# Hybrid encoder layer on Trainium2: twelve gate projections moved into attention, softmax row sums taken from a block of ones

## The reference

```
z = rms_norm(x) @ w_in          # -> c_q 256 | c_kv 128 | k_r 32 | u 1024 | gate_a 1024 | gate_b 1024
q = rms_norm(c_q) @ w_q_b       # 16 heads x (64 + 32 rotary), normalised per head, rotated
kv = [past, rms_norm(c_kv)] @ w_kv_b     # 16 heads x (64 key + 64 value), keys normalised per head
attn = softmax(q k^T / sqrt(96), block causal, chunk 64) @ v           # branch A
u_c = causal conv of width 4 over u
r, i = sigmoid(u_c @ w_rg + b_rg), sigmoid(u_c @ w_ig + b_ig)          # 8 blocks of 128
a = exp(-8 r softplus(-lam));  h_t = a_t h_(t-1) + sqrt(1 - a_t^2) (i u_c)_t    # branch B
x = x + (sigmoid(gate_a) * attn + sigmoid(gate_b) * h) @ w_out
x = x + ConvFFN(rms_norm(x))    # w_up to 5632, conv of width 3, silu gate, w_down
```

## Time and profile before

| what | us |
|---|---|
| median of three runs (945.2, 946.52, 2200.45) | 946.52 |
| the profiled execution's own time | 945.21 |
| span of the profiled execution | 943.3 |
| TensorE busy | 899.4 (95%) |
| TensorE weight loads busy (beside the matmuls) | 847.8 (90%) |
| VectorE busy | 604.8 (64%) |
| ScalarE busy | 347.5 (37%) |
| GpSimd busy | 238.3 (25%) |

### The profile page before, as it was taken

One profiled execution on the slowest core, in us unless ns is written; L12 is line 12 of the kernel. 1 busy time (PEld: TensorE's weight loads), 2 busy tenths in 40 slices (PEclk: granted clock), 3 DMA queues, 4 the chain that ended last, 5 costly groups with the idle time before them and its releaser, 6 DMA issues.

```text
span 943.3 us, 18508 instructions
## 1 busy us (share of the span) xinstructions
PE 899.4 (95%) x6689; PEld 847.8 (90%) x6689; DVE 604.8 (64%) x1182; ACT 347.5 (37%) x619; POOL 238.3 (25%) x278
## 2 busy tenths in 40 slices
PE   5999999998799999998999999999999999999998
PEld 5899999987577887776799999999999999999998
DVE  4378634686789888897544488777778777322221
ACT  6331455364344444442423533333333332112111
POOL 4000233462333221331012233333333333201000
PEclk8999999999899999997999999999999999999999
DMA  8333323322000000010003232233332222233321
GB/s 256 79 84 76 97 78 82 77 73 46 15 7 10 14 14 14 20 27 1 1 23 90 67 110 78 81 88 89 89 89 82 78 85 84 84 97 104 98 70 36
DMA packets 114630, 63.55 MB, mean 67 GB/s; under 512 B 7836, under 2 KB 113054, under 8 KB 114588
## 3 DMA queue, kind: packets, MB, share of 16 engines
q1 hardware_dynamic: 112396, 59.17, 22.4%
q0 software_dynamic: 2192, 3.81, 1.8%
HBM read 59.85 MB, written 2.70 MB: 66 GB/s over the span
## 4 chain that ended last, share of the span: by engine, by line
PE 86%; DVE 6%; issue 4%; ACT 2%; POOL 1%; SPq 1%; DMA 0%; DVEq 0%; ACTq 0%; POOLq 0%
PE PS L1141 61%; PE PS L1354 4%; PE PS L1338 4%; PE PS L1319 3%; PE PS L1176 3%; PE PS L1265 2%; PE PS L1308 2%; PE PS L1214 2%; PE PS L1261 1%; PE PS L1362 1%; PE PS L1292 1%; PE PS L1283 1%; DVE small L1010 1%; DVE w_lo L773 0%; PE PS L1325 0%
## 5 line engine op out<-in xcount | busy, mean ns | idle before, releaser
L541 ACT ACTIVATE w_hi<-w_raw 128x1024 fp32r<-128x1024 f32 (+2 forms) x104 | 107.6, 1035 | 368.7 <-PE PS L1141 354.4
L773 DVE TENSOR_TENSOR w_lo<-w_raw,w_hi 128x1024 fp32r<-128x1024 f32 (+2 forms) x104 | 128.1, 1231 | 122.8 <-ACT w_hi L541 122.6
L1141 PE MATMUL PS<-x2h,w_hi 128*128 128x274 f32 x704 | 147.7, 291 | 1.1 <-DVE w_lo L773 1.1
L1141 PE MATMUL PS<-x2h,w_lo 128*128 128x274 f32 x704 | 146.9, 290 | 0.0
L1141 PE MATMUL PS<-x2l,w_hi 128*128 128x274 f32 x704 | 146.9, 290 | 0.0
L1141 PEld LDWEIGHTS PS<-x2h,w_hi 128*128 128x128 f32 x704 | 111.9, 189 | 1.4 <-issue 1.3
L1141 PEld LDWEIGHTS PS<-x2l,w_hi 128*128 128x128 f32 x704 | 112.0, 189 | 0.0
L1141 PEld LDWEIGHTS PS<-x2h,w_lo 128*128 128x128 f32 x704 | 111.4, 189 | 0.0
L1141 PE MATMUL PS<-xnh,w_hi 128*128 128x274 f32 x384 | 83.3, 299 | 4.4 <-DVE w_lo L773 2.3
L1141 PE MATMUL PS<-xnl,w_hi 128*128 128x274 f32 x384 | 81.7, 295 | 0.0
L1141 PE MATMUL PS<-xnh,w_lo 128*128 128x274 f32 x384 | 81.0, 293 | 0.0
(11 more groups left out here) (254 smaller groups left out, 1706.6 us busy)
## 6 DMA issues: line engine op xcount, KB each, us to landing
w_raw<-in_w_up_dram SPq DMA_DIRECT2D x44, 512.0 KB, 3.8
w_raw<-in_w_in_dram SPq DMA_DIRECT2D x24, 512.0 KB, 3.9
w_raw<-in_w_down_dram SPq DMA_DIRECT2D x16, 512.0 KB, 3.7
w_raw<-in_w_out_dram SPq DMA_DIRECT2D x8, 512.0 KB, 4.1
w_raw<-in_w_down_dram SPq DMA_DIRECT2D x8, 384.0 KB, 3.9
xnat<-in_x_prompt_dram SPq DMA_DIRECT2D x4, 512.0 KB, 5.0
w_raw<-in_w_in_dram SPq DMA_DIRECT2D x4, 416.0 KB, 4.7
wq<-in_w_q_b_dram SPq DMA_DIRECT2D x8, 192.0 KB, 2.5
```

The source lines that it names most:

```text
L541: nc.scalar.activation(hi[:, slot % 2, 0:n], raw[:, slot % 4, 0:n], ACT.Copy).then_inc(s_hi, 1)
L773: tt(lo[:, slot % 2, 0:n], raw[:, slot % 4, 0:n], hi[:, slot % 2, 0:n].bitcast(F32), ALU.subtract).then_inc(s_lo, 1)
L1141: last = mm(PS[:, 2 * rank + j, 0:HT], w[:, slot % 2, cols], x[:, k0 + k, j * HT:(j + 1) * HT], start=(k0 + k == 0 and first), stop=(k0 + ...
```

## The change

The w_in items are reordered and split. Twelve stay ahead of attention (`FIRST`: gates A and B of block 0, the eight U, gates A and B of block 1). The twelve gate items of blocks 2 to 7 become fill inside attention: two a pair for the first five pairs, one for pairs 5 and 6. Each is done as two `gate_half`s of 24 matmuls, one half of the tokens each, in steps 3 and 4 (first item) and 7 and 8 (second). Gate sigmoids become tanh(x/2) on ScalarE with the factor 1/2 and the 1 added elsewhere.

The whole recurrence, with its LRU products, is moved to the stage of the U items. The first tap of the convolution is done by ScalarE. GpSimd's order there is written out: besides the recurrence it holds the squares and the rotation for pairs 0 and 1.

Row sums no longer come from ScalarE's accumulator. V has a third slot between its two heads, a block of ones; the stationary operand of a values matmul is one head's V and the ones, 128 columns, so the other head's 64 rows of PSUM receive the row sums. The reciprocal and the diagonal of every step are gone; the turn is a plain transpose against the identity, and waits for the exps. ScalarE copies the sums of a head out (`head_sums`), VectorE takes the reciprocal of 128 x 548 of them in two halves at steps 1 and 2 of the next pair (`sums_inverse`), and GpSimd multiplies and adds (`mix`).

In each step the turn and the values stand directly behind the scores, ahead of the fill. Scores use two banks in place of three. The attention loop is written out for all eight pairs. Of the w_out items the first two do seven of their eight blocks of k, then the last block each (in `output_product`).

```diff
-I_LAT, I_IN, I_OUT = 0, 4, 28
+FIRST = [("A", 0), ("B", 0)] + [("U", n) for n in range(KD)] + [("A", 1), ("B", 1)]
...
+def fills(p):
+    return [I_G + 2 * p, I_G + 2 * p + 1] if p < 5 else [I_G + 5 + p] if p < 7 else []
...
+            def gate_half(item, j):
+                pe.wait_ge(s_lo, item + 1)
+                for k in range(KD):
+                    cols = slice(k * P, (k + 1) * P)
+                    for w, x, first in ((hi, xnh, True), (hi, xnl, False), (lo, xnh, False)):
+                        last = mm(PS[:, j, 0:HT], w[:, item % 2, cols], x[:, k, j * HT:(j + 1) * HT],
+                                  start=(k == 0 and first), stop=(k == KD - 1 and w is lo))
+                last.then_inc(s_used if j else s_gp, 1)
...
-                pe.wait_ge(s_dg, p * 9 + (n + 1))
+                pe.wait_ge(s_e, p * 9 + (n + 1))
...
-                    last = mm(bank[:, a * P:(a + 1) * P], Pn[:, n % 3, a * P:(a + 1) * P], dg[:, n % 3, :], start=True, stop=True)
+                    last = nc.tensor.transpose(bank[:, a * P:(a + 1) * P], Pn[:, n % 3, a * P:(a + 1) * P], ident[:, :])
...
-                        last = mm(PS[h * VD:(h + 1) * VD, 3, t * P:(t + 1) * P], V[:, par, a, h, :], PT[:, b, a * P:(a + 1) * P],
-                                  start=(a == 0), stop=(a == t))
+                        last = mm(values_bank(h)[:, t * P:(t + 1) * P], V[:, par, a, h:h + 2, :].rearrange("p h n -> p (h n)"),
+                                  PT[:, b, a * P:(a + 1) * P], start=(a == 0), stop=(a == t))
...
+                    transpose_probs(p, n)
+                    if n:
+                        values(p, n - 1)
+                    if kq and n == 0:
...
+                    if following and n == 3:
+                        for v in range(2):
...
+                            transpose_kq(p + 1, v, v)
+                        pe.wait_ge(s_trf, 5 * (p + 1) + 1)
+                        gate_half(first, 0)
+                    if following and n == 4:
+                        pe.wait_ge(s_trf, 5 * (p + 1) + 2)
+                        gate_half(first, 1)
...
+                    if second and n == 7:
...
+                        gate_half(second, 0)
...
-                    transpose_probs(p, par, n)
-                    if n:
-                        values(p, par, n - 1)
...
+            def head_sums(p, h):
...
+                nc.scalar.activation(sums[rows(h), 0:SEQ], values_bank(h)[rows(1 - h), :], ACT.Copy).then_inc(s_sum, 1)
...
+            def sums_inverse(p, j):
...
+                ins = nc.vector.reciprocal(sums[:, cols], sums[:, cols])
...
+            for n in range(4, KD):
+                square_a(n)
+            rotate(0)
+            for n in range(4, KD):
+                lru_input(n)
+            squares_keys(1)
+            squares_queries(1)
...
             pool.wait_ge(s_rec, KD)
+            nc.gpsimd.memset(V[:, :, :, 1, :], 1.0).then_inc(s_clear, 1)
```

More of the change, by code:

```diff
@@ L139, in layer @@
         xT = fixed("xT", [P, KD, T])
-        rs_at = place
         rsT = fixed("rsT", [P, T])
@@ L369, in _ @@
+            for t in range(I_OUT + 6, I_UP):
+                w_out_item(t)
             with sp.Fori(0, NU // 4) as it:
@@ L1066, in _ @@
-            attend(6, 0)
-            attend(7, 1)
+            dve.wait_ge(s_rec, KD)
+            for p in range(NP_):
+                attend(p)
+            sums_inverse(7, 0)
+            sums_inverse(7, 1)
+            dve.wait_ge(s_ri, NP_)
+            o_p, h_p = gate("A", 7), U[:, 7, LEAD:]
+            dve.wait_ge(s_o, 3 * NP_)
+            link(tt(o_p, o_p, sums[:, :], ALU.mult))
+            dve.wait_ge(s_hb, NP_)
+            tt(h_p, h_p, o_p, ALU.add).then_inc(s_mix, 1)
+            mixed_lo(7)
@@ new lines, in _, with output_product @@
+            pe.wait_ge(s_rope4, 48)
+            pe.wait_ge(s_mask, 16 * 8)
+            scores(0, 0)
+            scores(0, 1)
+            pe.wait_ge(s_clear, 2)
+            for p in range(NP_):
+                attend(p)
+            def output_product(r, k0, nk):
+                for k in range(k0, k0 + nk):
+                    pe.wait_ge(s_ml, k + 1)
+                    cols = slice(k * P, (k + 1) * P)
+                    for w, x, first in ((hi, mxh, True), (hi, mxl, False), (lo, mxh, False)):
+                        for j in range(2):
+                            last = mm(PS[:, 2 * r + j, 0:HT], w[:, r, cols], x[:, k, j * HT:(j + 1) * HT],
+                                      start=(k == 0 and first), stop=(k == KD - 1 and w is lo))
+                return last
```

1037 lines of the change are left out of this document (603 added, 434 removed).

## The result

The changed kernel takes 976.6 us (median of four runs, 975.3 to 977.7) against 945.9 for the kernel before (one of whose four runs took 2200 and is left out of the ratio): 1.033 times as long, 95% interval 1.031 to 1.035. It is slower by 31 us. The forecast was 959.5, slower by 14 and most likely "no change"; the time lies inside the range of 917 to 978, at its upper end.

The account below looks back on a forecast made before the run. TensorE was taken to bound nearly everywhere, so gains come only where it stands. Attention's start 187.5, attention 302.8, the rest 465.4 and a 1.9 wait give 957.6 of span, plus 1.9 around it: 959.5 us, range 917 to 978.

Parts of the forecast that it names:

- the walk of 69.9 us: U stage, engine by engine from 116.3 to GpSimd's ones at 186.2; with 1.3 of half clock, attention begins at 187.5.
- product 8: Ninth of the twelve w_in products ahead of attention, numbered from 0 in FIRST order; forecast to begin at 116.3.
- the stop at product 2: Third w_in product: its w_lo stands behind latent norms and tiles on VectorE, put at 3.8 us.
- My check: End of U stage: GpSimd's own work of 37.3 us gives a floor of 169.4, with 17 us of waits in the walk.
- A pair: Attention, pair with two gate items: 38.8 us of TensorE work plus waits of 2.4 and 1.7, 42.9 us.
- VectorE's chain with the two reciprocals in it: Attention, pair start to first key columns: 14.1 us, against TensorE at the gate half after 11.7; wait 2.4.
- rival 2: Attention: VectorE and GpSimd hold each other up at the shared port, 2.5 us a pair, 977 us; chance 0.24.
- Pair 0: First attention pair, with no reciprocals: forecast at 42.1 us.
- product 10: Eleventh w_in product ahead of attention, in the U stage: forecast to begin at 133.7.
- The end of attention: w_out item 2 waits for item 0's last block and pair 7's mix, behind two reciprocals: 1.9 us; then 465.4 as before.
- Rival 1: U stage and attention: engines overlap better, attention starts near 173 and takes 278.8, total 919 us; chance 0.27.
- Rival 3: Attention: reciprocals take only 0.47 us, the first wait goes in five pairs, 948 us, no change; chance 0.11.

Follow-up runs that it names:

- tail2: Changed kernel with the end of the U stage reordered, and the recurrence of blocks 4 to 7 ahead of pair 0 on shared engines: 968.2 us, ratio 1.025.
- combined2: Changed kernel with U stage reordered as in tail2, gate B half first, later w_lo of second items, earlier w_lo for product 2, w_out reordered: 922.5 us, ratio 0.977.
- half-first run: Changed kernel with each pair's first gate half ahead of the turns of keys, the other turn ahead of the second half: 970.3 us, ratio 1.027.
- exps_early: Changed kernel with ScalarE's exps of blocks 0 to 3 at the end of step 7 of FIRST: 974.1 us, ratio 1.031.
- no_recip: Changed kernel with each reciprocal of the sums on one column in place of 274, output not divided by row sums: 953.6 us, ratio 1.009.

## Why the prediction went wrong

**The end of the U stage: the step that failed.** I let attention begin at 187.5; it was 200.8, which is 13.3 of the 18.3 us by which the span was missed. The term is the walk of 69.9 us from the start of product 8 to the ones; it measured 87.4. The start of product 8 was not at fault: it came 3 us earlier than forecast, although the stop at product 2 was 6.8 us and not 3.8. The account of the walk, counted from the start of product 8 (forecast 116.3, measured 113.3: it ended at 119.4): first input of the recurrence forecast +15.8, measured +24.0; last of the four scans +25.1 and +36.3; exps of blocks 4 to 7 begin +37 and +48.5; m2 of block 7 done +51.2 and +65.5; last scan +64.4 and +82.1; ones +69.9 and +87.4.

```profile
122.22 1.28 ACT L720 ACT_TABLE_LOAD   x1
```

```profile
137.34 6.80 POOL L512 TENSOR_TENSOR uc<-th,uc 128x548 f32<-128x548 f32 x4 [5.34 <-ACT th L726]
...
187.45 3.10 POOL L523 TENSOR_TENSOR kqs<-Kn 128x1152 f32<-128x1152 f32 x1
197.45 1.79 POOL L530 TENSOR_TENSOR kqs<-Qn 128x960 f32<-128x960 f32 x1 [6.90 <-DVE small L1070]
```

```profile
L1043 DVE TENSOR_TENSOR_SCAN U<-U,uc 128x548 f32<-128x548 f32 x8 | 13.4, 1679 | 0.3
L1035 DVE SCALAR_TENSOR_TENSOR th<-a,th 128x548 f32<-128x548 f32 x8 | 9.4, 1217 | 3.0 <-POOL a L507 3.0
L1045 DVE COPY st<-U 128x2 f32<-128x2 f32 x8 | 5.0, 626 | 0.3
```

```profile
188.69 1.89 DVE st L1045
```

Three errors of the walk show in it. The exps of blocks 0 to 3 stand behind the tap of step 8, so behind the end of product 8, at 122.2, where the tanh before them was done at 116.1 (6 us, of which moving them brought 2.6 at most). Some scans, copies and m2 beside GpSimd are much longer than alone. Three of the eight scans took 2.2 to 2.5 us, the other five 1.30; three of the eight copies of two columns took 1.1 to 1.9 us, the other five 0.17; the m2 have a mean of 1217 ns where undisturbed ones took 0.7 us: some 10 us in all, not all of it on the path (the last fence, from the chain of waits, is one such copy). I had put the port into a rival and given the rival attention as its place. And the last scans do not run beside the turn of pair 0 but behind the columns; GpSimd's squares for pair 1 then wait for sums that stand behind the scans, and the ones behind those squares. That both order and port matter, the runs show: with the order of `tail2` attention begins 6.5 us earlier, and the port cost 1.7 in one place. How the rest of the 13 us divides between them no run shows. My check, a floor of 169.4 from GpSimd's work alone, said little: attention began 31 us above it, not 17, and GpSimd's first input alone came 5 us later than the floor assumed.

**A pair: right in sum by luck, wrong in parts.** Forecast 42.9, measured 42.8. But the work is 36.6, not 38.8. The timelines of a pair before (28.4 us without its stop) and of pair 1 of `combined2`, each group counted from its start to the start of the next, show which terms were too large. The turns of the probabilities went from 6.2 to 2.8 us, so they saved 3.4 and not 2.8: the eight diagonal matmuls at 0.89 from which I took their price are cheaper than the mean of all. The 40 matmuls of `values` went from 5.5 to 4.3 us, though I had said that they cost what they did; the scores from 5.7 to 5.1. `values(8)` and the gate halves cost what I forecast (+1.1 and 12.5). Why a values matmul on 128 stationary columns is shorter here than one on 64 no run shows; the order is not it, as they still take 5.5 in the kernel before with the new order.

The stops and the clock make up the difference: 3.17 at the gate half (forecast 2.4), 1.6 of half clock behind it (forecast none), 1.38 (forecast 1.7, in step 4; it was in step 7, for a `w_lo`). The mechanism of the first, VectorE's chain with the two reciprocals in it, is borne out by the run without them. The chain took the 14.1 us that I gave it; TensorE was at the gate half after 11.0 and not 11.7. GpSimd's mix, which rival 2 suspected, is no cause of the stop, but the row of the half-first run shows that a wait for it lay hidden just behind.

Two figures of the forecast do not come out of its own rows. Pair 0, with no reciprocals to wait for, would by them be 38.8 + 1.7 = 40.5 and not 42.1 (it measured 41.2), and product 10, two steps of 8.0 behind product 8, would begin at 132.3 and not at 133.7, on which nothing else hangs.

**The end of attention.** The gap ahead of the third w_out item was forecast at 1.9; it was 3.46, and half clock behind it makes up the other 1.6 us of the 5.1 by which this part is longer than the 465.4 of before.

**The rivals.** Rival 1 (TensorE stays the bound) had 919, and `combined2` measured 922 with the order mended, but the agreement is in part luck: attention begins at 188.0 where the rival had 173, and takes 265.6 us where it had 278.8. Rival 2 had the right time for a wrong place. Rival 3 fell with the reciprocal's 1.85 us. By the Trainium skill's page VectorE: DVE Perf Modes, section First, the fixed hardware budget, I had estimated 2.3 us; the row decides, 1.85. Extended from the two small ones in the earlier trace rows it would have been 2.0, as far off as my 1.7 to the other side.

## What to carry to other kernels

Fill that is moved beside a chain of waits needs its own inputs and its own buffers to be early: list for each piece of fill the last thing on every engine that frees its bank, its slot and its operands, and start with the piece whose list is oldest. Price a stop of TensorE of 2 to 3 us with the clock behind it, and as a range, from nothing to the 3 us or so seen here. When a stage's work is taken away, the chain it covered (here the recurrence) becomes the stage; walk that chain by what each engine has queued ahead of each step, and put the engines that disturb each other into that walk and not into a rival.

## What the runs showed of the hardware that I had not expected

In the changed kernel's trace a stop of TensorE of 3.17 us was followed by 3.2 us at a granted clock of 0.50; in that of `exps_early` the same stop was followed by full clock in two of pairs 1 to 4. No stop of 1.17 us was followed by half clock in the pairs of `no_recip` (39.4 us, full clock). With the turn behind the fill, the same two stops (3.0 and 2.3 us) cost 1.6 us of clock in one pair and 4.5 in the next, in turn through pairs 1 to 4; what decides it was not tried. In the U stage a copy of two columns on VectorE took 1.89 us in place of 0.17 beside GpSimd's squares of 3.10, which themselves take 2.11 alone: both engines are longer, the small one by most of the other's instruction. In attention VectorE's reciprocal of 274 columns took 1.86 us both with GpSimd idle and beside its rotation, and leaving out GpSimd's mix, 2.3 us a pair, changed nothing. The reciprocal takes 6.8 ns an element over 274 columns. Forty fp32 matmuls with 128 columns of probabilities moving took 4.3 us with 128 stationary columns and 5.5 with 64.
